# One schedule edit in a two-layer transformer kernel: RWKV banks turned on by three, attention one step later, a weight split moved

## The chip, the cores and the metric

One Trainium2 chip, one of its cores. The metric is device time in microseconds (us) of one execution. TensorE (PE) does the matrix products and transposes, VectorE (DVE) and ScalarE (ACT) read its results and prepare its operands, GpSimd (POOL) does a few powers, SyncE (SP) issues the loads of weights.

## The reference, cut to what matters

```python
z = u @ w_in[i]                                   # attention, RWKV and gate columns
o_attn = dilated_attention_branch(z_attn)         # 3 groups x 4 heads, blocks of 128 queries
o_rwkv = rwkv7_time_mix(z_rwkv, ...)              # 8 heads of 64, a recurrence over 256 tokens
gate_attn, gate_rwkv = jnp.split(jax.nn.sigmoid(z_gate), 2, axis=-1)
merged = gate_attn * (o_attn @ w_attn_up[i]) + gate_rwkv * (o_rwkv @ w_rwkv_up[i])
h = h + rmsnorm(merged @ w_out[i], mix_post_norm[i])
...                                               # feed-forward, then a second block of another kind
```

The sequence has 256 tokens, the model 1024 features, everything is fp32. The change touches the first block only, between `z` and `merged`.

## The kernel before, in words

The kernel is one program in which each engine has a queue of its own, written out by Python generators. Each engine's program walks through the same generators (`qkv`, `gates`, `attention`, `rwkv`, `up3`), and `yield` ends a step. `turns.mix(fills(), rwkv(), order_1())` takes a main step for every "m" of the string that `order_1` gives and a step of RWKV for every "s"; `turns.paired(gates(), attention())` puts a step of attention behind each main step of the gates. All engines follow the same string, so the string sets the order on all four of them. Nothing is reordered on the chip: an engine takes its queue in order and waits on counts (`wait_ge`).

**Main steps.** A product with `w_in` in fp32 is made of three fp32r products (L717 to L719: high by high, high by low, low by high). Six matmuls, two of each line, are a main step (the gates have 32 of them, in four column blocks of 512: r = 2, 3, 0, 1). Their weights are split by ACT into a rounded half (L1786, 128x1024, two for each weight slot) and by DVE into the rest (L2643). The results are in PSUM banks 0 and 1, from which ACT reads them as tanh (L1782, `main_act "g1"`).

**Attention** runs for two blocks of queries i and two head pairs hh, in this order: scores (L1315, banks from the cycle 2, 3, 4: two banks for i = 0, three for i = 1); DVE reads them from PSUM with mask and minimum (L3023, a custom operation of DVE, `at_dve "r"`: two for i = 0, four for i = 1); ACT takes the exponential (L1783); DVE divides (L3030 and L2574, `at_dve "e"`); PE transposes (L723, tile `low,mid`, two steps); ACT copies; PE makes the output (L1358).

**RWKV** handles two chunks of 128 tokens. Its small steps on PE take their banks from another cycle, 4, 5, 6, 7 (`rw_bank`). Bank 4 is in both cycles. The last level of the triangular inverse is L1190 and its neighbours; then come L1212 and L1224; then for chunk 0 `state(0)`: right side (L1240), u (L1254), y and the carried state (L1265 to L1281). For chunk 1 come `received(1)` (L1118) and `keyed(1, 0)` (L1131) in one step, `keyed(1, 1)` in the next, and then `state(1)`. The normed output is transposed by `normed(i)` (L723, tile `low,high`, 4 transposes; called yt0 and yt1 below). DVE copies the right side and u (L2961, L2965), masks the products of L1118 and L1131 (L2915, L2922), multiplies the carried state (L2975), and does the sums of the normalization (L2865 to L2887).

**The end of the stretch.** `up3("a")` makes o_attn @ w_attn_up in 4 pieces of 6 matmuls in banks 0 and 1 (a00, a01, a10, a11 below, lines L1378 to L1380), `up3("r")` makes o_rwkv @ w_rwkv_up in 4 pieces of 12 matmuls in the RWKV banks. The weights of `r` are four tiles of 128x1024 (k = 0 to 3), each split by ACT (`up_wh`) and then by DVE (L3057, `up_columns`). DVE reads each piece of `a` with L2577 (`read_a`), and a10 and a11 wait until a00 and a01 have been read, since they use their banks again. After that `turn_parts("wo1")` transposes the merged rows (L723) in banks 5 and 6, and `block("wo1")` (L876, L877) goes on with w_out.

Of the kernel before, what the change touches and what calls it, by code (L numbers as in the profile page):

```python
# [276 lines left out]
def program(nc, A, consts, vecs, pt, out):  # L277
    with ExitStack() as ctx:
# [55 lines left out]
        def const(off, n):  # L334
            return low[:, OC + off:OC + off + n]
# [213 lines left out]
              "wo2": (A["w_out_2"][0], [P + 26152, P + 28200, P + 19968, P + 17920], m2Hi, m2Lo)}  # L549

        def order_1():
            return itertools.chain("msmsm" * 12, "msmsmms", "mms" * 10, "ms" * 4, "mms" * 7, "ms", "mms" * 6, "m" * 14, itertools.cycle("ms"))

# [148 lines left out]
        def tensor_program(e, turns):  # L704
# [291 lines left out]
            def rwkv():  # L996
# [154 lines left out]
                def chain():  # L1151
# [74 lines left out]
                    free[b] = [rw_act.at("x21", 1)]  # L1226
                    yield

                def state(i):
                    b = next(rw_bank)  # L1230
                    o = bank(b)
# [12 lines left out]
                    t.then_inc(rw_pe.up("rhs", i), 1)  # L1244
                    free[b] = [rw_dve.at("rhs", i)]
                    yield
                    b = next(rw_bank)
                    o = bank(b)
                    q.wait_ge(*rw_pool.at("ua", i))
# [50 lines left out]
                yield from up3("r", 4, rw_bank)  # L1300

            def attention():
                yield
                for i in range(2):
                    for hh in range(2):
# [54 lines left out]
                        t.then_inc(at_pe.up("o", i, hh), 1)  # L1360
                        free[b] = [at_act.at("o", i, hh)]
                        yield
                for _ in range(7):
                    yield

            def up3(tag, K, ring):
# [406 lines left out]
        def scalar_program(e, turns):  # L1773
# [205 lines left out]
            def rwkv():  # L1979
# [122 lines left out]
                def state(i):  # L2102
                    next(rw_bank)
                    yield
                    next(rw_bank)
                    yield
                    y_banks.append(bank(next(rw_bank)))
                    if i == 0:
                        next(rw_bank)
                    yield  # L2110
# [16 lines left out]
                yield from rwkv_up()  # L2127

            def attention():
                yield  # L2130
                for i in range(2):
                    for hh in range(2):
                        W, nb = 128 * (i + 1), 3 * (i + 1)
                        for _ in range(i + 2):
                            next(pa)
                        for par in range(2):
                            q.wait_ge(*at_dve.at("r", i, hh, par, i))
                            s = at_sm[par][:, 0:3 * W]
                            act(s, s, ACT.Exp, scale=-1.0, bias=sm_at[par][0][:, i:i + 1], accum=sm_at[par][1]) \
                                .then_inc(at_act.up("x", i, hh, par), 1)  # L2140
                        yield
                        yield
                        for par in range(2):
                            for b0 in range(0, nb, 4):
                                k = min(4, nb - b0)
                                p = bank(next(pa))
                                q.wait_ge(*at_pe.at("t", i, hh, par, b0))
                                copy(at_eT[par][:, 128 * b0:128 * (b0 + k)], p[:, 0:128 * k]).then_inc(at_act.up("t", i, hh, par, b0), 1)
                            yield
                        yield  # L2150
                        p = bank(next(pa))
                        q.wait_ge(*at_pe.at("o", i, hh))
                        copy(o_attn[:, hh, 128 * i:128 * i + 128], p[:, 0:128]).then_inc(at_act.up("o", i, hh), 1)
                        yield
                over = at_pe.at("o", 1, 1)
                up_rows("a", 0, 2, at_act.at("o", 1, 1))
                yield
                for k in range(2):
                    up_columns("a", k, over)
                    yield  # L2160
                yield
                up_rows("r", 0, 1, over, rw_dve.at("o", 0))
                yield
                for k in range(2):
                    up_columns("r", k, over)
                    yield

            def up_columns(tag, k, over):

                q.wait_ge(*landed(tag, k // 2))  # L2170
                q.wait_ge(*over)
                copy(up_wh[tag][k], slot(held(tag, k // 2))[:, 1024 * (k % 2):1024 * (k % 2) + 1024]).then_inc(up_act.up(tag, "w", k), 1)
# [11 lines left out]
            def up_a():  # L2184
                for n in range(4):
                    if n < 2:
                        up_columns("r", 2 + n, at_pe.at("o", 1, 1))
                    yield

            ups = up_a()  # L2190
# [373 lines left out]
        def vector_program(e, turns):  # L2564
# [3 lines left out]
            def bank(b):  # L2568
                return PSUM[:, b, :]
# [204 lines left out]
            def rwkv():  # L2774
# [183 lines left out]
                def state(i):  # L2958
                    o = bank(next(rw_bank))
                    q.wait_ge(*rw_pe.at("rhs", i))  # L2960
                    e.tensor_copy(RHS, o).then_inc(rw_dve.up("rhs", i), 1)  # L2961
                    yield
                    o = bank(next(rw_bank))
                    q.wait_ge(*rw_pe.at("u", i))
                    e.tensor_copy(U, o).then_inc(rw_dve.up("u", i), 1)  # L2965
# [33 lines left out]

            def attention():  # L3000
                ma = const(C_MA, 768)
                yield
                for i in range(2):
                    for hh in range(2):
# [42 lines left out]
                yield  # L3047
                up_rows("r", 0, 1)
                yield
                up_columns("r", 0)  # L3050
                yield

            def up_columns(tag, k):

# [9 lines left out]
            def up_a():  # L3064
                reads = up("a", [main_act.at("g1", 1, 1)], read_a)
                for n in range(4):
                    if n < 3:
                        up_columns("r", 1 + n)
                    next(reads)
                    yield  # L3070
# [825 lines left out]
```

## Time and profile before

| | before |
|---|---|
| median of 3 runs | 926.79 us (926.22 to 926.84) |
| the profiled execution | 926.23 us |
| its span | 924.4 us, so 1.8 us lie around the span |
| PE busy | 903.4 us, 98% of the span |
| DVE, ACT, POOL busy | 598.1, 447.6, 44.4 us |
| the chain that ended last | PE 87%, DVE 7%, ACT 2%, issue 2%, DMA 1% |
| granted clock, mean | 0.998 |

A share of 98% says that PE is the engine to watch and that only two kinds of time can be saved: time in which PE waits, and time in which its steps are longer than they must be. In the rows below, a number in square brackets is how long the engine stood idle ahead of the row, and what released it; start times are from the start of the span.

### The profile page before, as it was taken

The numbers are of one execution on the slowest core, as the hardware profiler recorded it, in microseconds if no ns is written. First come the engines' busy times: TensorE is split into PE (matmuls) and PEld (weight loads), VectorE is DVE, ScalarE is ACT, GpSimd is POOL, SyncE is SP. The second block draws the span as 40 slices with busy tenths as digits, with TensorE's granted clock in tenths as the row PEclk, the third lists the DMA queues.
The fourth block names the chain that finished last, engine by engine and source line by source line (L and its number), as shares of the span: only waits on it lengthen the run. The fifth ranks groups of instructions, "written<-read, shape, count | busy, mean of one in ns | idle before, by whom it ended". The sixth has DMA issues, their size and how long they took to land.

```text
span 924.4 us, 15532 instructions
## 1 busy us (share of the span) xinstructions
PE 903.4 (98%) x6632; PEld 761.9 (82%) x6632; DVE 598.1 (65%) x956; ACT 447.6 (48%) x724; POOL 44.4 (5%) x61
## 2 busy tenths in 40 slices
PE   7999999998999999999999999999999999999997
PEld 4999988777789988888889978776778798888885
DVE  4568977556855566656764577876863456666673
ACT  4775444436433444546443356483522445555571
POOL 0010000010000000000000440000000000000000
PEclk9999999999999999999999999999999999999999
DMA  9535333223667655555339674352626566665531
GB/s 336 183 122 153 95 99 101 80 92 95 225 249 238 218 182 183 185 202 203 115 115 212 144 225 151 111 182 92 226 92 205 138 182 182 183 185 187 204 108 45
DMA packets 131204, 150.78 MB, mean 163 GB/s; under 512 B 11808, under 2 KB 102176, under 8 KB 131008
## 3 DMA queue, kind: packets, MB, share of 16 engines
q1 hardware_dynamic: 129920, 145.57, 50.9%
q10 hardware_dynamic: 1216, 4.23, 1.2%
q8 instruction: 52, 0.85, 0.4%
q14 instruction: 16, 0.13, 0.0%
HBM read 148.73 MB, written 1.05 MB: 162 GB/s over the span
## 4 chain that ended last, share of the span: by engine, by line
PE 87%; DVE 7%; ACT 2%; issue 2%; DMA 1%; POOL 0%; POOLq 0%; ACTq 0%; DVEq 0%
PE psum L828 11%; PE psum L717 9%; PE psum L718 9%; PE psum L719 9%; PE psum L829 6%; PE psum L780 6%; PE psum L800 4%; PE psum L801 3%; PE psum L809 3%; PE psum L723 3%; PE psum L876 3%; PE psum L877 2%; PE psum L886 2%; PE psum L831 2%; PE psum L1683 1%
## 5 line engine op out<-in xcount | busy, mean ns | idle before, releaser
L1786 ACT ACTIVATE parts<-low 128x1024 fp32r<-128x1024 f32 (+3 forms) x246 | 248.3, 1044 | 81.5 <-PE psum L719 57.3
L2643 DVE TENSOR_TENSOR parts<-low,parts 128x1024 fp32r<-128x1024 f32 (+3 forms) x150 | 180.3, 1229 | 30.1 <-ACT parts L1786 29.9
L717 PE MATMUL psum<-parts 128*128 128x512 f32 (+2 forms) x424 | 170.3, 402 | 1.0 <-DVE parts L2643 1.0
L718 PE MATMUL psum<-parts 128*128 128x512 f32 (+2 forms) x424 | 164.0, 387 | 0.0
L719 PE MATMUL psum<-parts 128*128 128x512 f32 (+2 forms) x424 | 164.0, 387 | 0.0
L828 PE MATMUL psum<-parts 128*128 128x512 f32 x434 | 155.7, 398 | 0.0
L829 PE MATMUL psum<-parts 128*128 128x256 f32 x496 | 129.1, 281 | 0.0
L1786 ACT ACTIVATE high<-psum 128x512 f32<-128x512 f32 (+5 forms) x93 | 51.3, 563 | 150.6 <-PE psum L831 72.7
L829 PEld LDWEIGHTS psum<-parts 128*128 128x128 f32 x496 | 93.6, 189 | 5.7
L717 PEld LDWEIGHTS psum<-parts 128*128 128x128 f32 x424 | 80.0, 189 | 21.3 <-issue 3.1
L828 PEld LDWEIGHTS psum<-parts 128*128 128x128 f32 x434 | 81.7, 188 | 17.0
L719 PEld LDWEIGHTS psum<-parts 128*128 128x128 f32 x424 | 80.1, 189 | 16.5
L718 PEld LDWEIGHTS psum<-parts 128*128 128x128 f32 x424 | 80.2, 189 | 14.9 <-issue 0.7
L2706 DVE TENSOR_TENSOR parts<-low,parts 128x1024 fp32r<-128x1024 f32 x54 | 66.0, 1222 | 34.9 <-ACT parts L1786 34.9
L800 PE MATMUL psum<-parts 128*128 128x256 f32 (+2 forms) x296 | 78.8, 302 | 0.0
L801 PE MATMUL psum<-parts 128*128 128x256 f32 (+2 forms) x296 | 72.8, 282 | 0.0
L800 PEld LDWEIGHTS psum<-parts 128*128 128x128 f32 (+2 forms) x296 | 55.7, 188 | 4.8 <-issue 3.8
L780 PE MATMUL psum<-low 128*128 128x128 f32 x512 | 58.2, 275 | 0.4 <-DVE low L2620 0.4
L780 PEld LDWEIGHTS psum<-low 128*128 128x128 f32 x512 | 57.8, 192 | 0.8 <-issue 0.6
L801 PEld LDWEIGHTS psum<-parts 128*128 128x128 f32 (+2 forms) x296 | 55.9, 189 | 2.3 <-issue 2.2
L3136 DVE TENSOR_TENSOR mid<-psum,high 128x512 f32<-128x512 f32 x31 | 21.4, 692 | 44.8 <-ACT high L1786 44.8
L3580 POOL TENSOR_TENSOR low<-low 128x1 f32<-128x1 f32 x20 | 11.0, 552 | 640.0 <-DVE low L2574 563.3
(322 smaller groups left out, 1355.3 us busy)
## 6 DMA issues: line engine op xcount, KB each, us to landing
low<-in_w_in_dram SPq DMA_DIRECT2D x40, 1024.0 KB, 5.2
low<-in_w_ffn_in_dram SPq DMA_DIRECT2D x44, 512.0 KB, 5.2
low<-in_w_ff_in_dram SPq DMA_DIRECT2D x16, 1024.0 KB, 5.6
low<-in_w_ff_out_dram SPq DMA_DIRECT2D x16, 1024.0 KB, 4.9
low<-in_w_ffn_out_dram SPq DMA_DIRECT2D x11, 1024.0 KB, 4.9
low<-in_w_out_dram SPq DMA_DIRECT2D x8, 1024.0 KB, 5.2
low<-in_w_ple_gate_dram SPq DMA_DIRECT2D x4, 1024.0 KB, 5.0
low<-consts_dram ACTq DMA_DIRECT2D x1, 2142.0 KB, 9.2
```

The source lines that it names most:

```text
L717: mm(o, l[0], r[0], start, False)
L718: mm(o, l[0], r[1], False, False)
L719: return mm(o, l[1], r[0], False, stop)
L723: return e.transpose(o, a, low[b:b + n, OC + C_ID + b:OC + C_ID + b + n])
L780: t = mm(PSUM[0:m, banks[n], 256 * j + 128 * i:256 * j + 128 * i + 128], w3[:, k, off:off + m], uT[:, k, 128 * i:128 * i + 128], k == 0, k ...
L800: mm(o, hi[:, k, c], st.uh[:, k, :], k == 0, False)
L801: mm(o, lo_[:, k, c], st.uh[:, k, :], False, False)
L828: mm(p, hi[:, k, c], st.u2(k), k == 0, False)
L829: mm(p[:, 0:256], lo_[:, k, c], st.uh[:, k, :], False, False)
L1786: return e.activation(o, a, ACT.Copy)
L2643: tt(rslot3(n, nk, width)[:, r, 0:w], slot3(n, nk, width)[:, r, 0:w], st.hi3(j)[:, r, 0:w].bitcast(F32), ALU.subtract) \
L2706: tt(rview(OR + 2048 * n + 1024 * (k % 2), 1024), slot(n)[:, 1024 * (k % 2):1024 * (k % 2) + 1024], rview(base, 1024).bitcast(F32), ALU.su ...
```

## The change

It has four parts. (1) `order_1` is rewritten from the 12th "mms" on, so that some RWKV steps come earlier or later between the main steps. (2) `attention` has one more empty step at its start and one fewer at its end, on every engine: each of its steps stands one main step later. (3) In `state(1)` three banks of `rw_bank` are skipped before u, on every engine: u, y, yt0, yt1 and the four pieces of `up3("r")` are in other banks than before (yt0 in bank 7, was 4; the pieces in 5, 6, 7, 4, were 6, 7, 4, 5). (4) The splits of w_rwkv_up, k = 0 and 1 on ACT and k = 0 on DVE, leave the tail of `attention` and stand in `up_a`, beside the pieces of `up3("a")`. No instruction is added or removed, and nothing changes outside this stretch.

```diff
@@ -549,7 +549,8 @@
               "wo2": (A["w_out_2"][0], [P + 26152, P + 28200, P + 19968, P + 17920], m2Hi, m2Lo)}
 
         def order_1():
-            return itertools.chain("msmsm" * 12, "msmsmms", "mms" * 10, "ms" * 4, "mms" * 7, "ms", "mms" * 6, "m" * 14, itertools.cycle("ms"))
+            return itertools.chain("msmsm" * 12, "msmsmms", "mms" * 10, "ms" * 5, "mmmmmms", "ms", "mms" * 2, "ms", "mms", "ms",
+                                   "mms" * 2, "ms" * 3, "mms", "m" * 6, itertools.cycle("ms"))
 
 
 
@@ -1226,6 +1227,11 @@
                     free[b] = [rw_act.at("x21", 1)]
                     yield
 
+                def apart_from_scores(i):
+                    if i == 1:
+                        for _ in range(3):
+                            next(rw_bank)
+
                 def state(i):
                     b = next(rw_bank)
                     o = bank(b)
@@ -1244,6 +1250,7 @@
                     t.then_inc(rw_pe.up("rhs", i), 1)
                     free[b] = [rw_dve.at("rhs", i)]
                     yield
+                    apart_from_scores(i)
                     b = next(rw_bank)
                     o = bank(b)
                     q.wait_ge(*rw_pool.at("ua", i))
@@ -1300,6 +1307,7 @@
                 yield from up3("r", 4, rw_bank)
 
             def attention():
+                yield
                 yield
                 for i in range(2):
                     for hh in range(2):
@@ -1360,7 +1368,7 @@
                         t.then_inc(at_pe.up("o", i, hh), 1)
                         free[b] = [at_act.at("o", i, hh)]
                         yield
-                for _ in range(7):
+                for _ in range(6):
                     yield
 
             def up3(tag, K, ring):
@@ -2102,7 +2110,8 @@
                 def state(i):
                     next(rw_bank)
                     yield
-                    next(rw_bank)
+                    for _ in range(4 if i == 1 else 1):
+                        next(rw_bank)
                     yield
                     y_banks.append(bank(next(rw_bank)))
                     if i == 0:
@@ -2127,6 +2136,7 @@
                 yield from rwkv_up()
 
             def attention():
+                yield
                 yield
                 for i in range(2):
                     for hh in range(2):
@@ -2161,9 +2171,7 @@
                 yield
                 up_rows("r", 0, 1, over, rw_dve.at("o", 0))
                 yield
-                for k in range(2):
-                    up_columns("r", k, over)
-                    yield
+                yield
 
             def up_columns(tag, k, over):
 
@@ -2184,7 +2192,8 @@
             def up_a():
                 for n in range(4):
                     if n < 2:
-                        up_columns("r", 2 + n, at_pe.at("o", 1, 1))
+                        for k in range(2):
+                            up_columns("r", 2 * n + k, at_pe.at("o", 1, 1))
                     yield
 
             ups = up_a()
@@ -2960,6 +2969,9 @@
                     q.wait_ge(*rw_pe.at("rhs", i))
                     e.tensor_copy(RHS, o).then_inc(rw_dve.up("rhs", i), 1)
                     yield
+                    if i == 1:
+                        for _ in range(3):
+                            next(rw_bank)
                     o = bank(next(rw_bank))
                     q.wait_ge(*rw_pe.at("u", i))
                     e.tensor_copy(U, o).then_inc(rw_dve.up("u", i), 1)
@@ -2999,6 +3011,7 @@
 
             def attention():
                 ma = const(C_MA, 768)
+                yield
                 yield
                 for i in range(2):
                     for hh in range(2):
@@ -3047,8 +3060,6 @@
                 yield
                 up_rows("r", 0, 1)
                 yield
-                up_columns("r", 0)
-                yield
 
             def up_columns(tag, k):
 
@@ -3064,6 +3075,8 @@
             def up_a():
                 reads = up("a", [main_act.at("g1", 1, 1)], read_a)
                 for n in range(4):
+                    if n == 0:
+                        up_columns("r", 0)
                     if n < 3:
                         up_columns("r", 1 + n)
                     next(reads)
```

**On PE**, where the scores of the second query block stand (L1315 before, L1323 after, the change having moved the lines). Before, for hh = 0 and then, further on, for hh = 1:

```order
L1315 MATMUL psum<-mid 128x256 [waits attn_act,rwkv_dve]
L1315 MATMUL psum<-mid 128x256 x4
L1315 MATMUL psum<-mid 128x256 [waits attn_pe]
L1240 MATMUL psum<-high 64x64 x2
...
L1315 MATMUL psum<-mid 128x256 [waits attn_act]
L1315 MATMUL psum<-mid 128x256 x4
L1315 MATMUL psum<-mid 128x256 [waits attn_pe]
L723 MATMUL psum<-low,high 128x128 [waits rwkv_dve,attn_dve]
L723 MATMUL psum<-low,high 128x128 x3
```

Now, for i = 0 hh = 1, i = 1 hh = 0, and i = 1 hh = 1:

```order
L1323 MATMUL psum<-mid 128x128 x6
L1119 MATMUL psum<-high 128x128 [waits attn_dve]
L1119 MATMUL psum<-high 128x128 x7
...
L1323 MATMUL psum<-mid 128x256 [waits attn_pe]
L1132 MATMUL psum<-high 128x256 [waits attn_dve]
L1132 MATMUL psum<-high 128x256 x3
...
L1323 MATMUL psum<-mid 128x256 [waits attn_pe]
L724 MATMUL psum<-low,high 128x128 [waits rwkv_dve]
L724 MATMUL psum<-low,high 128x128 x3
```

The wait on `attn_dve` has left yt0 (L723, now L724). `received(1)` (L1118, now L1119) and `keyed(1, 1)` (L1131, now L1132) have moved directly behind scores, and each of them now has such a wait.

**On DVE**, between the reading of the scores i = 0 hh = 1 (L3023, now L3036) and their division (L3030 and L2574, now L3043 and L2583). Before:

```order
L3023 ISA mid,low<-psum,low 128x384 [waits attn_pe]
L3023 ISA low 128x1
L2975 TENSOR_TENSOR high<-psum,low 64x4x64 [waits rwkv_pool,rwkv_pe]
L2975 TENSOR_TENSOR high<-psum,low 64x4x64
L3030 RECIPROCAL low<-low 128x1 [waits attn_act]
L2574 TENSOR_SCALAR mid<-mid,low 128x384 [waits attn_dve]
```

Now:

```order
L3036 ISA mid,low<-psum,low 128x384 [waits attn_pe]
L3036 ISA low 128x1
L2924 TENSOR_TENSOR high<-psum,low 128x4x128 [waits rwkv_pe] x2
L2931 TENSOR_TENSOR high<-psum,low 128x512 [waits rwkv_pe] x2
L2874 TENSOR_REDUCE low<-high 128x8 [waits rwkv_act]
L2583 TENSOR_SCALAR low<-low 128x8 [waits rwkv_dve]
L2878 TENSOR_TENSOR high<-high,low 128x512 [waits rwkv_dve]
L2652 TENSOR_TENSOR parts<-low,parts 128x1024 [waits split_act]
L3043 RECIPROCAL low<-low 128x1 [waits attn_act]
L2583 TENSOR_SCALAR mid<-mid,low 128x384 [waits attn_dve]
```

Eight instructions now stand ahead of the division: the masking of L1118 and L1131, three of the normalization and a weight split (the carried state has gone ahead of the scores).

**On ACT, then DVE**, at the last gates and the `up` products. ACT before (L1782 on `mid` are the two last tanh, L1782 on `high` reads yt1, L1786 on `parts<-low` behind the tanh are the splits of w_rwkv_up, k = 0, 1, 2, 3):

```order
L1782 ACTIVATE mid<-psum 128x512 [waits main_pe]
L1786 ACTIVATE parts<-low 128x1024 [waits slot_in2]
L1786 ACTIVATE parts<-low 128x1024
L1782 ACTIVATE mid<-psum 128x512 [waits main_pe]
L1786 ACTIVATE parts<-low 128x1024 [waits slot_in4]
L1782 ACTIVATE high<-psum,low 128x128 [waits rwkv_pe]
L1782 ACTIVATE high<-psum,low 128x128 x3
L1786 ACTIVATE parts<-low 128x1024
```

ACT now (lines 1782 and 1786 are now 1790 and 1794):

```order
L1790 ACTIVATE mid<-psum 128x512 [waits main_pe]
L1794 ACTIVATE parts<-high 128x4x128
L1790 ACTIVATE high<-psum,low 128x128 [waits rwkv_pe]
L1790 ACTIVATE high<-psum,low 128x128 x3
L1790 ACTIVATE mid<-psum 128x512 [waits main_pe]
L1794 ACTIVATE parts<-low 128x1024 [waits slot_in2]
L1794 ACTIVATE parts<-low 128x1024
L1794 ACTIVATE parts<-low 128x1024 [waits slot_in4]
L1794 ACTIVATE parts<-low 128x1024
```

DVE now, at the same place (L3068 are the splits of k, L2586 on `high` the reads of a00, a01; L2894 and L2896, which were L2885 and L2887, finish the second chunk's output):

```order
L3068 TENSOR_TENSOR parts<-low,parts 128x1024 [waits up_act] x2
L2586 SCALAR_TENSOR_TENSOR high<-mid,psum 128x512 [waits main_act,up_pe]
L2894 TENSOR_TENSOR high<-high 128x4x128 [waits rwkv_act]
L2896 TENSOR_TENSOR high<-high 128x4x128 [waits rwkv_dve]
L3068 TENSOR_TENSOR parts<-low,parts 128x1024 [waits up_act]
L2586 SCALAR_TENSOR_TENSOR high<-mid,psum 128x512 [waits up_pe]
```

All splits of w_rwkv_up now stand behind the last tanh on ACT, and behind the read of yt1. On DVE the two splits ahead of the read of a00 have stayed, and L2885 and L2887 have come between the reads of a00 and a01 (before, they stood behind the third read).

## Rows read from the trace of the kernel before

**Rows 1.** The page, busy time: engine, us (share of the span), instructions.

```profile
PE 903.4 (98%) x6632; PEld 761.9 (82%) x6632; DVE 598.1 (65%) x956; ACT 447.6 (48%) x724; POOL 44.4 (5%) x61
```

**Rows 2.** Waits of PE, whole span: us in total, times, longest.

```profile
PE psum L723 <- DVE low L3023: 2.4, 1, 2.4
...
PE psum L1315 <- DVE mid L2753: 0.8, 1, 0.8
PE psum L723 <- DVE mid L2574: 0.6, 1, 0.6
```

**Rows 3.** Timeline of PE, 170 to 224 us: start, duration, count, [idle before].

```profile
170.94 0.94 PE L1315 MATMUL psum<-mid 64*128 64x128 f32 x12
...
178.09 1.16 PE L1118 MATMUL psum<-high 64*128 64x128 f32 x16
...
180.29 0.50 PE L717 MATMUL psum<-parts 128*128 128x512 f32 x1
...
188.68 1.67 PE L1315 MATMUL psum<-mid 64*128 64x256 f32 x12
...
209.06 1.67 PE L1315 MATMUL psum<-mid 64*128 64x256 f32 x12
213.08 0.72 PE L723 MATMUL psum<-low,high 128*128 128x128 f32 x4 [2.35 <-DVE low L3023]
...
217.93 0.82 PE L723 MATMUL psum<-low,mid 128*128 128x128 f32 x6
...
220.53 0.47 PE L717 MATMUL psum<-parts 128*128 128x512 f32 x1
...
223.47 1.53 PE L1358 MATMUL psum<-mid 128*64 128x128 f32 x24
```

**Rows 4.** Windows: us, busy of PE, PEld, DVE, ACT, POOL, then granted clock.

```profile
214.00:215.00 1.00, 1.00 (x4) 0.77 (x3) 0.79 (x2) 1.00 (x5) 0.00 (x0) 0.50 0.00 0
```

**Rows 5.** Timeline of DVE, 171 to 214 us.

```profile
171.91 0.56 DVE L3023 CUSTOM_DVE_ANT_1 mid<-psum,low 128x384 f32<-128x384 f32 x1 [1.75 <-PE psum L1315]
...
183.21 1.22 DVE L2643 TENSOR_TENSOR parts<-low,parts 128x1024 fp32r<-128x1024 f32 x1
...
190.28 0.69 DVE L3023 CUSTOM_DVE_ANT_0 mid<-psum,low 128x512 f32<-128x512 f32 x1 [3.06 <-PE psum L1315]
...
191.89 0.75 DVE L3023 CUSTOM_DVE_ANT_0 mid<-psum,low 128x512 f32<-128x512 f32 x1
...
192.56 0.69 DVE L2961 COPY high<-psum 128x512 f32<-128x512 f32 x1
...
213.18 0.62 DVE L2574 TENSOR_SCALAR mid<-mid,low 128x768 f32<-128x768 f32 x1
```

**Rows 6.** Timeline of PE, 234 to 254 us.

```profile
234.63 0.39 PE L1378 MATMUL psum<-parts 128*128 128x512 f32 x1
...
238.59 0.50 PE L1378 MATMUL psum<-parts 128*128 128x512 f32 x1
...
240.32 0.50 PE L1378 MATMUL psum<-parts 128*128 128x512 f32 x1
...
253.73 1.06 PE L723 MATMUL psum<-low,high 128*128 128x128 f32 x8 [0.87 <-DVE mid L2577]
```

**Rows 7.** Timeline of ACT, 234 to 240 us.

```profile
234.49 2.01 ACT L1786 ACTIVATE parts<-low 128x1024 fp32r<-128x1024 f32 x2 [1.79 <-DMA low<-in_w_rwkv_up_dram]
236.40 0.58 ACT L1782 ACTIVATE mid<-psum 128x512 f32<-128x512 f32 x1
...
238.00 1.49 ACT L1782 ACTIVATE high<-psum,low 128x128 f32<-128x128 f32 x4
```

**Rows 8.** Timeline of DVE, 235 to 244 us.

```profile
235.58 2.36 DVE L3057 TENSOR_TENSOR parts<-low,parts 128x1024 fp32r<-128x1024 f32 x2 [2.65 <-ACT parts L1786]
237.86 0.68 DVE L2577 SCALAR_TENSOR_TENSOR high<-mid,psum 128x512 f32<-128x512 f32 x1
...
242.21 0.69 DVE L2885 TENSOR_TENSOR high<-high 128x512 f32<-128x512 f32 x1
```

## The prediction

> **What bounds the kernel.** I began with the page's busy times: PE works 98% of the span [rows 1], so only PE's own waits and stretched steps can change the time. The view of PE's waits, second, shows how few there are: the largest inside the program is one of 2.35 us, then 0.8 and 0.6 [rows 2], and 0.87 where the merged rows are transposed [rows 6]. Third, the timeline places the largest: it stands ahead of the four transposes of yt0, right behind the scores i = 1, hh = 1 [rows 3]. These scores fill banks 2, 3, 4; yt0 wants bank 4, which DVE reads last of the three. The reader should see a second loss behind it: from 213.08 to 217.93 PE made 4 transposes and 12 matmuls in 4.85 us, while 12 matmuls alone take 2.94 us (220.53 to 223.47) [rows 3]. With 0.4 for the transposes that is 1.5 us too long, and the granted clock was 0.50 there [rows 4]: half of full speed, 1.2 in place of 2.4 GHz. So this wait costs 2.35 + 1.5.
>
> **What the change removes.** (a) yt0 goes to bank 7, its wait on DVE is gone, and with it the slow stretch: -3.85. (b) The first scores come one main step (1.4 us) later, behind L1190, so that their rope sum is ready: -0.8. (c) The division of i = 1, hh = 0 now has `keyed(1, 1)`, the right side and two main steps in front of the transposes that need it: -0.6. (d) The transposes of the merged rows use banks 5 and 6. Before, bank 5 belonged to the last piece of `up3("r")` and had to be read first; now banks 5 and 6 belong to its first two: -0.87. The load of w_out's last part, which starts at the end of that piece, would be the next thing late there; its transfer and its two splits have 0.87 us less before they are needed. I find them just in time and count the whole 0.87; at worst it is given back there. (e) PE changes the shape of its tile (128*128, 64*128, 128*64, 64*64 in the rows) less often: small steps that stood as 64*128 next to 64*64 or 128*64 now stand alone or beside their own shape. I count 33 changes of shape before and 30 now in this stretch. Twelve matmuls between transposes and a 64-wide step took 2.94 us [rows 3], against 54 in 12.54 us of `up` work (240.32 to 252.86) [rows 6], 2.79 for twelve: 0.15 for both ends. Three changes at 0.1 are -0.3, with 0 and -0.45 as ends. Together: -6.4.
>
> The Trainium skill (TensorEngine Tiling (Array Packing), Key Properties) says that changing the tiling mode drains TensorE. It gives no figure. This case's rows agree that there is a cost, and put it at 0.15 us or less; if this rule were all that counts, the change would be a gain of up to 0.45 us.
>
> **What it adds.** Five waits, each worked out from rows.
>
> (f) `received(1)`, L1118, now follows the scores i = 0, hh = 1 directly and takes banks 7 and 4; the scores took 4 and 2. It waits for DVE's first read. Scores started at 170.94, that read at 171.91 and lasted 0.56 [rows 3, 5]: with 0.1 to hand over, 1.6 us from the scores' start, of which the scores themselves are 0.9. Wait 0.7.
>
> (g) The division for i = 0, hh = 1 stands behind eight more instructions on DVE. From L1118's start (178.09) to the end of the weight split (183.21 + 1.22) is 6.3 us [rows 3, 5]; reciprocal and division of 384 columns, 0.6 (below the 0.62 + 0.2 that 768 need), give 6.9. PE meanwhile has L1118 and L1131, 2.2 us (178.09 to 180.29) [rows 3], and two main steps, 2.95: 5.15. Its transposes wait 1.75. Queued behind them are all later main steps; nothing else on PE can go first.
>
> (h) `keyed(1, 1)`, L1131, follows the scores i = 1, hh = 0 and takes banks 7 and 4; the scores have 3, 4, 2. It waits for the third read. DVE starts 1.6 us after the scores (188.68, 190.28), and the fourth read starts another 1.6 us later (191.89) [rows 3, 5]; the scores are over after 1.6. Wait 1.6.
>
> (i) For i = 1, hh = 1 a weight split comes between reads and division. Start of reads 1.6, four reads 2.3 (190.28 to 192.56) [rows 5], split 1.15, reciprocal and division 0.8 [rows 5]: 5.85 us. PE has scores 1.65, yt0 0.4, two main steps 2.85: 4.9. Wait 1.0.
>
> (j) The `up` products. ACT's tanh for the last main step stands ahead of all splits of w_rwkv_up, so that k = 0 starts 0.7 us after the main steps end (0.2 until the last matmul's result, which lasts 0.39 but is issued 0.23 behind its neighbour; 0.5 for the tanh of 0.58) [rows 6, 7]. From that start to the start of a10 took 4.1 us before (234.49 to 238.59) [rows 6, 7]: two splits on ACT and DVE, then the read of a00 (237.86) [rows 8]. That chain is the same now. From a10 to a11 were 1.7 us [rows 6]; now L2885 and L2887 (0.69 each, 1.3 with the handover) [rows 8] stand in between: 3.05. From a11 to the end of `up3("r")`, 252.86, were 12.55. Sum 20.4 us after the main steps, against 18.2 before (234.63 to 252.86) [rows 6]. Since yt1 (0.4) was inside the 18.2 and now stands ahead, the cost is 2.6. On PE it shows as waits of 2.05 ahead of a10 (a00 and a01 take 2.75) and 1.7 ahead of a11. Before, the load of w_rwkv_up held k = 0 until 234.49 [rows 7]; now it lands in time and would allow an earlier start, which the tanh ahead of it prevents.
>
> Costs 0.7 + 1.75 + 1.6 + 1.0 + 2.6 = 7.65. With the gains of 6.4 the sum is +1.2 us, give or take 0.8 for the lengths of the steps between (a main step takes 1.4 to 1.6 by its neighbours).
>
> **The open price: the clock.** The clock fell behind a wait of 2.35 us. Behind one of 0.87 it did not: eight transposes in 1.06 us there, four in 0.72 behind the long one [rows 3, 6]. The new waits of 1.6 to 2.05 lie between, so each may cost 0 or 1.5 us. In (j) much of a fall would be hidden, since a10 could take twice its 1.4 us while a11 waits for DVE anyway. (g) at 1.75 is nearer to 2.35 than to 0.87, (h) at 1.6 is in the middle. I take one fall, +1.5, and keep 0 and +4.5 as ends. Sum +2.7 us against the profiled execution's 926.23, so 928.9; that execution lies 0.56 below the median of the runs, at whose level the forecast is 929.5 us.
>
> **The rivals.** All times at the level of the median.
> - *No fall of the clock.* The five waits come, but at 1.75 us or a pair of 2.05 and 1.7 the clock holds. +1.2: 928.0. For it: PE is busy between the two waits of (j). Against: the half-speed stretch is as sure in the row as the wait ahead of it.
> - *Falls at two places or more.* +4.2 or more: 931.0. For it: three places lie between the known ends.
> - *The `up` products are not held back*, the way to "not slower". If k = 0 is split before the last tanh (or a10 and a11 do not wait for it), (j) is nothing: 1.2 - 2.6 = -1.4, 925.4, and with no fall of the clock still no faster than 0.2%. It decides from the point where ACT starts that split at the end of the main steps or earlier. Against: ACT's order as printed leaves no way past the tanh.
> - *The waits on bank 4 and on the divisions are smaller than I read*, because DVE begins its reads sooner after small scores, or PE comes later to them. With (f) to (i) at half, 2.5 us less: -1.3 without a fall, 925.5. Against: both scores with three banks show the same 1.6 us to the first read.
> - *The change doesn't do what it says*, and yt0 waits for its own data: its input comes from L2879, which stands ahead of the reads of these scores on DVE before and now, so this has no chance of its own.
>
> **Chances.** Forecast 0.38, no fall 0.32, two falls or more 0.12, `up` not held back 0.10, smaller waits 0.08. A measurement of this kernel can tell about 0.2%, 1.85 us, from no change. Slower by more than that: nearly all of the first, all of the third, a fifth of the second, 0.54. Faster by more: only where both of the last two rivals meet or an unseen gain is added, 0.07. Within: 0.39. The range leaves out a tenth at each end, 926.2 to 931.6 us; the forecast's own is 928.5 to 930.5.
>
> **What the profile after would show.** PE's wait of 2.35 at yt0 gone, and 0.87 at the merged transposes; waits on DVE at L1119 (0.7), at the transposes L724 of i = 0 hh = 1 (1.75), at L1132 (1.6), at L724 of i = 1 hh = 1 (1.0), and at the up products (2.05 and 1.7, put down to DVE). A granted clock of 0.50 at one of these places and not at 214 us. I am wrong if waits of more than 1.5 us are missing at L1132, whose length hangs on nothing but the reads; if a10 starts less than 3 us after the main steps; or if a wait appears that I don't name.

## The result, and the profile after

The changed kernel takes 928.25 us (median of 14 runs, 927.56 to 930.99), the kernel before 926.25 beside it: a ratio of 1.0028 with a 95% interval of 1.0021 to 1.0035, so 2 to 3 us slower. One run of the kernel before here and one of up_mended further down, of 1811.69 and 2301.97 us, were slow ones and are outside the ratios. The forecast was 929.5, with a chance of 0.54 on slower. In the profiled execution the span is 926.2 us against 924.4.

First the page's busy times, after:

```profile
PE 902.1 (97%) x6632; PEld 760.8 (82%) x6632; DVE 599.0 (65%) x956; ACT 447.0 (48%) x724; POOL 44.3 (5%) x61
```

The same instructions, 1.3 us less PE time than in [rows 1], and a longer span: PE's steps got shorter (mostly because this execution has no stretch at half clock, as is shown below) and its waits longer. The view of PE's waits from 170 to 258 us (us in total, times, longest), against [rows 2]:

```profile
PE psum L1386 <- DVE high L2586: 3.3, 2, 1.9
PE psum L724 <- DVE mid L2583: 2.5, 2, 1.6
PE psum L1132 <- DVE low L3036: 1.6, 1, 1.6
PE psum L1132 <- ACT high L1794: 0.7, 1, 0.7
PE psum L1119 <- DVE low L3036: 0.7, 1, 0.7
```

The 2.35 us of [rows 3], the 0.87 of [rows 6], the first scores' 0.78 and the 0.6 of (c) are gone, and seven waits stand in their place. The timeline of PE shows where (start, duration, count, idle before). L724 was L723, L1323 was L1315 and L1386 was L1378:

```profile
175.04 0.94 PE L1323 MATMUL psum<-mid 64*128 64x128 f32 x12
176.63 1.16 PE L1119 MATMUL psum<-high 64*128 64x128 f32 x16 [0.65 <-DVE low L3036]
178.44 1.14 PE L1132 MATMUL psum<-high 64*128 64x256 f32 x8 [0.66 <-ACT high L1794]
...
184.14 0.55 PE L724 MATMUL psum<-low,mid 128*128 128x128 f32 x3 [1.62 <-DVE mid L2583]
...
191.49 1.67 PE L1323 MATMUL psum<-mid 64*128 64x256 f32 x12
194.72 1.14 PE L1132 MATMUL psum<-high 64*128 64x256 f32 x8 [1.55 <-DVE low L3036]
...
213.53 1.67 PE L1323 MATMUL psum<-mid 64*128 64x256 f32 x12
215.13 0.66 PE L724 MATMUL psum<-low,high 128*128 128x128 f32 x4
215.54 0.48 PE L718 MATMUL psum<-parts 128*128 128x512 f32 x1
...
219.42 0.87 PE L724 MATMUL psum<-low,mid 128*128 128x128 f32 x6 [0.88 <-DVE mid L2583]
...
240.14 0.50 PE L1386 MATMUL psum<-parts 128*128 128x512 f32 x1 [1.91 <-DVE high L2586]
...
243.21 0.50 PE L1386 MATMUL psum<-parts 128*128 128x512 f32 x1 [1.40 <-DVE high L2586]
```

yt0 (215.13) follows its scores at once. Waits (f), (g), (h), (i) and the two of (j) are where the prediction put them. The one at 178.44 it didn't name: `keyed(1, 0)` takes bank 5, which holds Y of chunk 0, and ACT copies Y only behind two exponentials (the third row below is the copy). ACT, 176 to 179 us:

```profile
176.61 0.61 ACT L1791 ACTIVATE mid<-mid,low 128x384 f32<-128x384 f32 x1 [4.17 <-DVE low L3036]
...
177.22 0.60 ACT L1791 ACTIVATE mid<-mid,low 128x384 f32<-128x384 f32 x1
...
177.82 0.57 ACT L1794 ACTIVATE high<-psum 128x512 f32<-128x512 f32 x1
```

And (j) on DVE: L2894 and L2896 stand between the read of a00 (239.41) and that of a01 (242.47), for which a10 and a11 wait.

```profile
239.41 0.68 DVE L2586 SCALAR_TENSOR_TENSOR high<-mid,psum 128x512 f32<-128x512 f32 x1
240.00 0.69 DVE L2894 TENSOR_TENSOR high<-high 128x512 f32<-128x512 f32 x1
240.72 0.69 DVE L2896 TENSOR_TENSOR high<-high 128x512 f32<-128x512 f32 x1
241.33 1.22 DVE L3068 TENSOR_TENSOR parts<-low,parts 128x1024 fp32r<-128x1024 f32 x1
242.47 0.68 DVE L2586 SCALAR_TENSOR_TENSOR high<-mid,psum 128x512 f32<-128x512 f32 x1
```

The granted clock is 1.00 in every window from 170 to 256 us of this execution, so the fall that the forecast took isn't in this one.

**A ledger of the stretch.** From a product in front of the first moved step (L762 before, at 149.94 us; L763 after, at 150.07) to the transposes of the merged rows, PE does the same work in every kernel. I took the distance between the two starts and added up PE's idle times in between. The rest is work, together with gaps too short for the view to list.

| profiled execution | from, to | length | idle | rest |
|---|---|---|---|---|
| before | 149.94, 253.73 | 103.79 | 5.07 | 98.72 |
| after | 150.07, 255.59 | 105.52 | 8.67 | 96.85 |
| turn_only | 150.07, 250.13 | 100.06 | 2.96 | 97.10 |
| no_turn | 150.09, 257.95 | 107.86 | 11.02 | 96.84 |
| splits_back | 150.21, 255.25 | 105.04 | 7.99 | 97.05 |
| reads_first | 149.85, 254.03 | 104.18 | 7.27 | 96.91 |
| up_mended | 149.54, 253.25 | 103.71 | 6.59 | 97.12 |
| banks_clear | 150.08, 255.12 | 105.04 | 8.64 | 96.40 |
| one_apart | 150.45, 250.18 | 99.73 | 2.15 | 97.58 |

turn_only has before's order of instructions on PE and no clock fall: its rest is 1.62 us shorter than before's, which is the price of the fall at 214 us. after's is another 0.25 shorter, as (e) wants. But that doesn't show (e): the kernels with after's order on PE, all with the same 30 changes of shape, have rests from 96.40 to 97.12, and turn_only and one_apart, both with before's changes of shape, lie 0.48 apart. Differences below half a microsecond or so can't be told apart in the rest.

### The profile page after: what moved, and what is told of

It reads as the page before. It is cut to its first block, busy times and chain, and to the rows that moved or that the text cites. A ratio compares the mean times of both kernels' runs of the same rounds, so it can differ in the third digit from the quotient of the medians.

```text
span 926.2 us, 15530 instructions
## 1 busy us (share of the span) xinstructions
PE 902.1 (97%) x6632; PEld 760.8 (82%) x6632; DVE 599.0 (65%) x956; ACT 447.0 (48%) x724; POOL 44.3 (5%) x61
## 4 chain that ended last, share of the span: by engine, by line
PE 88%; DVE 7%; ACT 2%; issue 2%; DMA 1%; POOL 0%; POOLq 0%; ACTq 0%; DVEq 0%
PE psum L829 11%; PE psum L718 9%; PE psum L720 9%; PE psum L719 9%; PE psum L830 6%; PE psum L781 6%; PE psum L801 4%; PE psum L802 3%; PE psum L810 3%; PE psum L724 3%; PE psum L877 3%; PE psum L887 2%; PE psum L878 2%; PE psum L832 2%; PE psum L1691 1%
```

## The experiments

Each diff below shows the lines that matter of its edit, and the matching steps on the other engines follow them.

**Two groups of spans.** The spans of the kernel before fall into two groups: in the 59 executions that ran beside the experiments, 28 have 922.2 to 923.2 us and 31 have 923.7 to 924.8; none lies between. The profile that the prediction read is of the upper group. I call them lower and upper, and compare lower with lower where a kernel has both. The experiments ran in three batches, in each of which the lower group of before has its median at 922.7 or 922.8, so batches can be compared. after: 11 spans from 925.7 to 926.6 and 3 from 927.9 to 928.6.

The granted clock, averaged over a whole execution, goes with the groups: it is 0.998 or more in all 28 lower executions of before, and 0.996 to 0.998 in the upper ones. So a mean of 0.996 or 0.997 points to a fall, and 0.998 says nothing.

**turn_only.** Before, with the turn of the ring alone:

```diff
 # state(i), between the right side and u, on PE; the same on ACT and DVE
+                    apart_from_scores(i)      # if i == 1: three next(rw_bank)
```

> The kernel before with one part of the change alone: the second chunk's ring is turned three banks on behind its right side, so that yt0 takes bank 7 and not bank 4. Order, waits for weights and splits stay as before. My reading (a) and (d) says -3.85 for the wait of 2.35 us and the slow stretch behind it, and -0.87 at the merged rows: -4.7 us against before, ratio 0.995, with at most 1 us given back at the transposes of i = 1, hh = 1, whose division was ready only about 1 us after their new start. Rival: the loads of w_rwkv_up hold the up products at the same time as before, because DMA works at 0.9 of its share there; then the gain stops at the main steps and the sum is -0.9. Rival: the slow stretch belongs to the place and not to the wait; then -3.2.

Measured: 922.89 us, ratio 0.9974 (0.9963 to 0.9984); spans 920.2 to 921.1 in one group; 920.7 in the profile, 3.7 below the profile of before and 2.1 below before's lower group. The expectation of -4.7 against before was too large: against the profile, which has the fall, it is -3.7, and by the medians -2.5, since only about half of before's executions have the fall. The slow stretch isn't tied to its place, as it's gone with the wait; and the gain of the main steps came through, so the loads don't hold it back. 1.34 us are given back at the transposes of i = 1, hh = 1, not by their division but by ACT. Its timeline of PE:

```profile
210.74 0.66 PE L723 MATMUL psum<-low,high 128*128 128x128 f32 x4
214.00 0.82 PE L723 MATMUL psum<-low,mid 128*128 128x128 f32 x6
216.06 0.60 PE L723 MATMUL psum<-low,mid 128*128 128x128 f32 x4
217.99 0.44 PE L723 MATMUL psum<-low,mid 128*128 128x128 f32 x2 [1.34 <-ACT mid L1792]
```

And of ACT:

```profile
214.08 1.48 ACT L1788 ACTIVATE high<-psum,low 128x128 f32<-128x128 f32 x4
215.45 2.01 ACT L1792 ACTIVATE parts<-low 128x1024 fp32r<-128x1024 f32 x2
217.34 0.87 ACT L1792 ACTIVATE mid<-psum 128x512 f32<-128x512 f32 x2
```

The copy that frees the bank (217.34) stands behind two splits of a main step's weights (215.45). Idle time falls from 5.07 to 2.96, by 2.11, which is the 2.1 between the lower groups.

**wait_filled, wait_filled3.** Before, with eight or three extra matmuls in the wait for bank 4. Their result is used by nobody:

```diff
+                    if i == 0:                # normed(0), ahead of yt0
+                        o = bank(5)
+                        for n in range(8):    # 3 in wait_filled3
+                            mm(o[:, 0:256], st1.uh[:, n, 0:128], st1.uh[:, n, 0:256], True, True)
```

> The kernel before with eight extra matmuls (128x256, their result is used by nobody) in front of yt0, in the 2.35 us in which PE waits for bank 4; yt0 stays on bank 4. Some executions of the kernel before have a span of 922.2 to 923.0 us and some of 923.8 to 924.7. If this split is the clock, which falls behind the idle 2.35 us in some executions and not in others, then filled idle time keeps the clock up in all of them: span 922.6 in every execution, granted clock 1.00 behind yt0, median about 1 us below that of before. If the fall belongs to the place or comes by itself, both spans remain. If the matmuls last longer than the wait, their excess (up to 0.3 us) is added.

> The same with three extra matmuls: PE works some 0.7 us of the 2.35 and is idle for 1.6, as ahead of keyed(1, 1) in the changed kernel. If a wait of that length doesn't lower the clock, all spans are at 922.6 as with eight. If it does in some executions, the upper group at 924.2 stays, with fewer or as many members.

Measured: wait_filled 922.4 to 923.4 in all 11 executions, no upper group and no mean clock under 0.998 (median of the times 924.91 against 925.16, ratio 0.9994, 0.9985 to 1.0003; the expected gain of 1 us in the median didn't come, because 12 of before's 23 executions beside it were lower ones). wait_filled3: 7 spans of 922.3 to 923.1 and 4 of 924.2 to 924.5 (ratio 0.9999, 0.9990 to 1.0007). With eight, PE's timeline:

```profile
210.71 1.21 PE L1078 MATMUL psum<-parts 128*128 128x256 f32 x8
213.13 0.66 PE L723 MATMUL psum<-low,high 128*128 128x128 f32 x4 [1.21 <-DVE low L3027]
```

and a window behind it, with the granted clock as the third number from the end:

```profile
214.00:215.00 1.00, 1.00 (x6) 0.80 (x5) 0.79 (x2) 1.00 (x5) 0.00 (x0) 1.00 0.00 0
```

With three, the same two views:

```profile
210.86 0.63 PE L1078 MATMUL psum<-parts 128*128 128x256 f32 x3
213.28 0.66 PE L723 MATMUL psum<-low,high 128*128 128x128 f32 x4 [1.79 <-DVE low L3027]
213.69 0.65 PE L717 MATMUL psum<-parts 128*128 128x512 f32 x1
```

The window:

```profile
214.00:215.00 1.00, 1.00 (x4) 0.72 (x4) 0.65 (x3) 1.00 (x5) 0.00 (x0) 0.50 0.00 0
```

The wait for bank 4 ends at the same place in both. Behind 1.21 us of idle time no span of 11 is in the upper group. Behind 1.79 us the clock was at 0.50 (1.2 GHz) in this execution, and 4 of 11 spans carry the price. Behind 2.35 us, 31 of 59 do. So the two groups are the clock: filling the wait takes the upper one away. At the lengths of 1.79 and 2.35 us the same kernel falls in one execution and not in the next, and no run shows what decides it.

**no_turn.** after without the turn, the opposite of turn_only:

```diff
-                    apart_from_scores(i)      # and the same turn on ACT and DVE
```

> The changed kernel without the turn of the ring: yt0 is on bank 4 again. By my (a), yt0 waits 2.35 us behind the scores; it covers the division of i = 1, hh = 1, whose wait of 0.88 goes; by (d) the merged rows wait up to 0.87 us again. Sum +1.5 to +2.3 us against the changed kernel's 926.2 span, so 927.7 to 928.5, and up to 1.5 more in executions in which the clock falls. If the turn were worth what it is worth in the kernel before without the clock (turn_only against the lower group of spans, -1.9 us), +1.9.

Measured: spans 928.0 and 928.5, and three of 929.8 to 930.0: the two of the lower group are 2.1 above that of after. Idle time grows by 2.35 (ledger), with no fall in this execution although the wait of 2.35 is back: +2.35 at yt0, -0.88 at the division that it covers, +0.87 at the merged rows. The ratio to before is 1.0067 (1.0053 to 1.0080).

**splits_back, reads_first, up_mended.** Two edits in the up products of after, alone and together. splits_back: ACT splits the first two parts of w_rwkv_up ahead of the last tanh again. reads_first: L2894 and L2896 come behind the read of a01.

```diff
 # splits_back, ACT, last step of attention's tail (and DVE's first split with it; up_a gives them up)
+                for k in range(2):
+                    up_columns("r", k, over)
 # reads_first, DVE, up_a
                     next(reads)
+                    if n == 1:
+                        gated(1)              # L2894 and L2896, taken out of normed(1)
```

> The changed kernel with its last part alone undone: the first two parts of w_rwkv_up are split on ACT ahead of the last tanh again (ACT order: two splits, tanh, two splits). If the whole of (j) hangs on this part, -2.6 us against the changed kernel, ratio to before about 1.000. If only the 0.7 us of the tanh hangs on it, and the rest of (j) comes from the two gating steps L2894 and L2896 that stand between the reads of a00 and a01, then the wait ahead of a10 shrinks from 1.9 to 1.2 us, the wait ahead of a11 stays at 1.4, and the time falls by 0.7 us.

> The changed kernel with the two gating steps on DVE (L2894, L2896) behind the read of a01 in place of ahead of its split. If they set the start of a11, its wait of 1.4 us goes and the time falls by 1.35 us against the changed kernel. If the wait ahead of a11 is set by the split of w_rwkv_up's third part, nothing changes. If ACT, which waits for the gated rows ahead of w_out's splits, is late behind them, the 1.35 us comes back as waits at the first block products.

> Both edits of splits_back and reads_first on the changed kernel. Of (j)'s 2.6 us the one took 0.5 (spans 925.6 against 926.1 of the changed kernel's lower group) and the other 1.45 (924.7 in its lower group). If they are two links in a row, a10 waits 1.2 us, a11 nothing, and the lower group of spans is at 924.2. If both shorten the same stretch, it stays at 924.7. Rival: with an earlier start of the up products ACT, which waits for the gated rows, is late for w_out.

Measured medians of the spans, lower group, against 926.2 of after: splits_back 925.6 (-0.6; 7 executions), reads_first 924.7 (-1.5; 6 of 11), up_mended 924.1 (-2.1; 10 executions; its ratio to before is 1.0004, 0.9995 to 1.0014). The lengths in the ledger say nearly the same: -0.48, -1.34 and -1.81. In splits_back ACT starts the first split behind the four scalings of yt1, only 0.36 us sooner than in after (235.68, 236.04), and the tanh then comes two splits later (237.57). The two edits are links in a row and add up. With reads_first the wait at a11 is gone from the view and the 1.91 at a10 stays; in up_mended that one is 1.23.

**reads_first_b, reads_first_c.** The kernel of reads_first again, for a profile of its upper group (spans of 925.8 to 926.6).

> reads_first once more, for a profile of an execution of its upper group (5 of its 11 spans were 925.8 to 926.6, the others 924.4 to 924.8). If the upper group is a clock fall, the profile of such an execution shows a stretch with a granted clock of 0.50 behind one of the waits of 1.5 to 1.9 us: ahead of a10 by my (j), where here no second wait hides it, or at the division (g) or keyed(1, 1) (h). In an execution of the lower group the clock is 1.00 all through and this run tells nothing.

> The same kernel again, for the same reason: a span of 925.8 or more comes with a stretch at 0.50 behind one of the three waits, a span of 924.8 or less with none.

Measured: spans 926.4 and 924.8. The one of 926.4 shows the fall, behind the wait at a10; its matmuls go from 0.23 us apart to 0.43. The timeline of PE in that execution:

```profile
240.19 0.50 PE L1386 MATMUL psum<-parts 128*128 128x512 f32 x1 [1.91 <-DVE high L2586]
...
240.76 0.50 PE L1388 MATMUL psum<-parts 128*128 128x512 f32 x1
241.06 0.63 PE L1386 MATMUL psum<-parts 128*128 128x512 f32 x1
241.49 0.63 PE L1387 MATMUL psum<-parts 128*128 128x512 f32 x1
```

The window behind it, clock 0.50:

```profile
242.00:243.00 1.00, 1.00 (x4) 0.81 (x3) 0.96 (x2) 0.00 (x0) 0.00 (x0) 0.50 1.05 387
```

In after the clock may fall here too, but there PE waits 1.40 us for a11 right behind, which would hide much of it. The mean clocks point that way: it is 0.996 not only in the 3 upper executions of after but in 2 of the 11 lower ones as well (926.2 and 926.4), and 0.996 or 0.997 in 4 of the 6 of banks_clear below, whose spans are no longer than the others. None of these executions was profiled, so where the clock fell in them, and where the 3 upper ones lose their 2 us, isn't shown. splits_back and up_mended have no wait above 1.62 us in this stretch, and none of their 17 executions has an upper span or a mean clock under 0.998: nothing shows that waits like (g) and (h) bring a fall.

**banks_clear.** after with `received(1)` and `keyed(1, 1)` off bank 4:

```diff
                 def second():
+                    for _ in range(3):
+                        next(rw_bank)
                     received(1)
                     keyed(1, 0)
                     yield
                     keyed(1, 1)
+                    next(rw_bank)
```

> The changed kernel with received(1) on banks 6 and 7, keyed(1, 0) on 4 and 5, keyed(1, 1) on 6 and 7, and everything behind as it is. If (f) and (h) are costs that add up, -0.7 and -1.6: -2.3 us against the changed kernel. If a wait that is taken away only uncovers the next one, the 0.65 us of (f) turns into a longer wait of keyed(1, 0) for the copy of Y on ACT (0.66 now, 1.3 then), or into a longer wait of the transposes of i = 0, hh = 1 for their division, which does not come sooner, and only (h) is won: -1.6 us. With (h) gone the division of i = 1, hh = 0 may be late by up to 1 us instead.

Measured: 927.91 us; spans 925.6 to 926.3, median 925.8: -0.4 where -1.6 or -2.3 was expected. Its view of PE's waits:

```profile
PE psum L1132 <- ACT high L1797: 1.7, 1, 1.7
PE psum L1246 <- DVE high L2934: 1.2, 1, 1.2
```

Both waits for the scores' reads are gone, and two others hold PE to nearly the same moments: `keyed(1, 0)` starts at 178.54 (178.44 in after), since it waits 1.67 for Y's copy, and the right side (L1246) starts at 196.87 (197.36 in after), since it waits 1.19 us for DVE's masks of `keyed(1, 1)` (L2934). These start at 195.44 us, when DVE is through with its four reads; in after they start at 195.88. Both expectations failed: (f) gave nothing, and of (h)'s 1.55 about 0.4 was won. It is DVE and ACT that are late here, and the bank was only the first place to feel it.

**one_apart.** turn_only with a main step more between the two blocks of transposes of i = 1, hh = 1, and one turn fewer in attention's tail:

```diff
                            yield
+                            if (i, hh, par) == (1, 1, 0):
+                                yield
```

> turn_only with one more main step between the two blocks of transposes of i = 1, hh = 1, and one turn fewer in attention's tail. In turn_only PE waits 1.34 us there for ACT, whose copy of the first block stands behind two splits for a main step. If only that copy is late, the wait goes and the span falls from 920.7 to about 919.4 us. If attention's later end makes the split of w_attn_up late, the gain comes back as a wait ahead of the up products.

Measured: 922.75 us, ratio 0.9972 (0.9961 to 0.9982), spans 920.2 to 920.7: 0.2 below turn_only, not 1.3. The 1.34 us is gone and 0.32 is left behind it, which makes 1.02 less. Counted from the start of the ledger's stretch, PE comes to the up products only 0.54 us sooner; the rest went in gaps that the view doesn't list. There the wait at a10 grows from 0.19 to 0.42, since the first split of w_rwkv_up starts at the same time. ACT's timeline in one_apart:

```profile
231.96 2.01 ACT L1794 ACTIVATE parts<-low 128x1024 fp32r<-128x1024 f32 x2 [1.77 <-DMA low<-in_w_rwkv_up_dram]
```

and in turn_only:

```profile
231.88 2.01 ACT L1792 ACTIVATE parts<-low 128x1024 fp32r<-128x1024 f32 x2 [1.53 <-DMA low<-in_w_rwkv_up_dram]
```

The loads were issued at 226.86 and 227.02, and in both kernels ACT's idle time ahead of the split ends with the landing. So the loads, which didn't hold back turn_only's gain, are the next bound. These two are the fastest kernels of the study, 0.26% and 0.28% under before.

## Why the prediction was right, and where it wasn't

**The gains.** (a) is right as a mechanism and, in executions in which the clock falls, in size: 2.35 + 1.62 where 3.85 was said. What failed is that it was taken from one profile as a fixed sum: the 1.5 belongs to 31 of 59 executions of before. (b) 0.78 and (d) 0.87 came in full, and (c) 0.63. For (e) 0.3 was said, and the rest in the ledger is 0.25 shorter, which is within its scatter. The Trainium skill (TensorEngine Tiling (Array Packing), Key Properties) says that TensorE is drained at a change of tiling mode and gives no figure; no run here shows what the three changes saved are worth. Sum: 4.63 of idle time, 1.62 and 0.25, so 6.5 against 6.4.

**The costs.** (f) 0.65 against 0.7, (g) 1.62 against 1.75, (h) 1.55 against 1.6, (i) 0.88 against 1.0: each within 0.13. Missing from the list was the 0.66 us at `keyed(1, 0)`, which I had said would prove me wrong: the walk followed the ring against DVE's reads and didn't look up which ACT instruction frees bank 5. (j): the waits are 3.31 us, of which 0.44 was there before (237.03), so 2.87 against 2.6. The prediction's working has both causes in it: 1.35 for L2894 and L2896 between the reads (3.05 against 1.7), where reads_first gives 1.5, and the later start of the splits, where splits_back gives 0.6. The first of them comes from the order of RWKV's steps, not from the fourth part of the change; about 0.8 is left with both undone. The costs come to 8.2 against 7.65.

**The net.** Without any clock fall in after: -6.5 + 8.2 = +1.7 in the profiled executions (105.52 - 103.79, and +1.8 of span) against +1.2. That is inside the 0.8 given: costs too low by 0.6, gains by 0.1.

**The open price.** The step that failed is "I take one fall, +1.5". The typical execution of after doesn't pay for one (11 of 14 spans), though it has a wait of 1.91 us, behind which the clock fell in reads_first_b, and behind 1.79 us it fell in 4 of 11 executions. If the mean clocks say here what they say of before, a fall came in at least 5 of the 14, and 2 of these have a span of the lower group: the fall that much of (j) hides, which the prediction had named, would look like that. I asked which wait is too long, as if there were one answer; the runs show a chance behind each of the long ones (2.35, 1.91, 1.79) and no sign of one at 1.62 or less. The likeliest case of the forecast was thus not the one that came, and the rival without a fall, at 928.0, is nearest to the measured 928.25. The forecast's 929.5 was 1.25 too high. 0.54 of that is its starting point, a median of 926.79 where the 14 runs have 926.25. The other 0.7 is an increase of 2.7 where 2.0 was measured: 1.5 for the fall that mostly wasn't paid, against a net that was 0.5 too low in the profiles (1.7) and 0.3 more by the medians (2.0). That errors of both signs met is luck. By groups the change costs more than the ratio says: lower against lower it is 926.2 against 922.7, +3.5 us across batches (+2.9 by the device times within the first), and the ledger gives +3.6 of idle time less 0.25. The median of before sat in its upper group where after's sat in its lower.

**The rivals.** *Not held back* took the whole of (j) for the tanh: with the split ahead of it 0.6 is won, not 2.6. In the result its condition isn't met, the first split starts behind the tanh (236.04). *Smaller waits* is out, the waits are as long as read. *Doesn't do what it says* is out by yt0's missing wait, turn_only and no_turn.

## What to carry to other kernels

Of the four parts one was worth having. The turn of the ring costs no instruction and saves 2.1 us by itself, and the fourth part costs 0.6. The new order of the steps and attention's step later were never run one without the other, so how the rest of the loss divides between them isn't shown; together with the fourth part they filled the stretch with waits for engines that are late. Undo such an edit part by part before judging it as a whole. A wait on a buffer may be only the first of several ways to feel one late engine: price it by what stands behind the same engine's next result, as banks_clear shows. And where a profile holds a clock fall, look first at the spans of the other executions, to see in how many of them it happens.

## What the runs showed of the hardware

TensorE's granted clock fell from 2.4 to 1.2 GHz behind idle times of 2.35, 1.91 and 1.79 us inside a stretch of dense matmuls, but only in a part of the executions of one and the same kernel: 31 of 59 at 2.35 us, 4 of 11 at 1.79. Behind 1.21 us it fell in none of 11, and in the 17 executions of splits_back and up_mended, with waits up to 1.62 us, there is no sign of a fall. A fall cost 1.62 us in before (ledger, against turn_only), 1.25 in reads_first_b (105.43 between the ledger's two starts, against 104.18 in reads_first_c), and 1.5 by the medians of before's two groups. The Trainium skill (TensorE: Matmul & The Clock Gate, Part 1: The HAM clock gate) says that the number of slow matmuls at a kernel's start varies from run to run. Here the same kernel varies in its middle too, in whether there is a fall at all. The filled wait is a cure where the wait itself can't be removed: eight matmuls without use took the upper group away, and their median span, 922.9, is within 0.2 of before's lower group.
